# Smaller first transfers with four matmuls on a cleared tile, and later scores, in a two-layer hybrid mixer kernel on one core

## The reference

```python
h = rms_norm(x, pre_g)
proj = h @ w_in              # 2048 x 24576: twelve sections of 1536 columns, three gates of 2048
o_a = dilated_mixture_attn(q_a, k_a, v_a) * silu(z_a)       # 12 heads x 128
o_c = b_c * causal_short_conv(c_c * u_c, conv_w, conv_b) * silu(z_c)
o_r = retention(rotary(q_r), rotary(k_r), v_r) * silu(z_r)  # 12 heads x 128, then normed
merged = sigmoid(g_a) * (o_a @ w_branch_a) + sigmoid(g_c) * (o_c @ w_branch_c) \
       + sigmoid(g_r) * (o_r @ w_branch_r)
x = x + rms_norm(merged @ w_out, post_g)
```

## Time and profile before

| | |
|---|---|
| median of 3 runs | 2788.71 us (2786.34 to 2789.78) |
| the profiled execution | 2791.59 us, its span 2789.7 us |
| PE busy | 2753.0 us (99%) |
| DVE busy | 1845.4 us (66%) |
| ACT busy | 1229.3 us (44%) |
| DMA | 529.11 MB, mean 190 GB/s |

### The profile page before, as it was taken

One profiled execution on the slowest core, in us unless ns is written; L12 is line 12 of the kernel. 1 busy time (PEld: TensorE's weight loads), 2 busy tenths in 40 slices (PEclk: granted clock), 3 DMA queues, 4 the chain that ended last, 5 costly groups with the idle time before them and its releaser, 6 DMA issues.

```text
span 2789.7 us, 30530 instructions
## 1 busy us (share of the span) xinstructions
PE 2753.0 (99%) x12360; PEld 2282.8 (82%) x12360; DVE 1845.4 (66%) x2431; ACT 1229.3 (44%) x1426; POOL 28.2 (1%) x35
## 2 busy tenths in 40 slices
PE   8999999999999999999999999999999999999998
PEld 7888888888888878888878888888888888788887
DVE  5677644767655797746567776447776557877464
ACT  5454544444443333344454545444444433343443
POOL 0000000000000000000000000000000000000000
PEclk9999999999999999999999999999999999999999
DMA  8555556555555555556565555565655564555663
GB/s 312 174 173 195 167 196 196 190 191 194 196 196 193 167 184 170 171 200 213 181 227 178 178 187 167 195 196 182 202 192 194 196 196 156 192 169 171 204 211 136
DMA packets 264108, 529.11 MB, mean 190 GB/s; under 512 B 8352, under 2 KB 8480, under 8 KB 263712
## 3 DMA queue, kind: packets, MB, share of 16 engines
q1 hardware_dynamic: 260208, 517.24, 56.4%
q10 hardware_dynamic: 2752, 5.05, 0.5%
q0 software_dynamic: 1008, 4.87, 0.5%
HBM read 522.94 MB, written 4.19 MB: 189 GB/s over the span
## 4 chain that ended last, share of the span: by engine, by line
PE 98%; issue 1%; DVE 0%; DMA 0%; ACT 0%; DVEq 0%; POOL 0%; ACTq 0%; POOLq 0%
PE ps L585 32%; PE ps L587 32%; PE ps L586 32%; PE ps L516 1%; PE ps L539 0%; PE ps L542 0%; PE ps L540 0%; PE ps L512 0%; PE ps L497 0%; PE ps L526 0%; PE ps L517 0%; PE ps L511 0%; DMA merged<-xT 0%; DVE gates L1082 0%; DVE hT_trail L1054 0%
## 5 line engine op out<-in xcount | busy, mean ns | idle before, releaser
L824 DVE TENSOR_TENSOR w_trail<-raw,w_lead 128x1024 fp32r<-128x1024 f32 x975 | 1191.6, 1225 | 885.1 <-ACT w_lead L644 877.8
L644 ACT ACTIVATE w_lead<-raw 128x1024 fp32r<-128x1024 f32 x975 | 1029.9, 1060 | 1455.7 <-PE ps L587 1445.9
L585 PE MATMUL ps<-w_lead,hT_lead 128*128 128x512 f32 x3328 | 1301.3, 391 | 10.2 <-DVE w_trail L1091 8.7
L587 PE MATMUL ps<-w_lead,hT_trail 128*128 128x512 f32 x3328 | 1296.1, 389 | 0.0
L586 PE MATMUL ps<-w_trail,hT_lead 128*128 128x512 f32 x3328 | 1295.8, 389 | 0.0
L585 PEld LDWEIGHTS ps<-w_lead,hT_lead 128*128 128x128 f32 x3328 | 625.7, 188 | 141.6 <-DVE hT_trail L1073 8.6
L587 PEld LDWEIGHTS ps<-w_lead,hT_trail 128*128 128x128 f32 x3328 | 625.4, 188 | 130.3
L586 PEld LDWEIGHTS ps<-w_trail,hT_lead 128*128 128x128 f32 x3328 | 625.8, 188 | 128.5
L585 PE MATMUL ps<-w_lead,oT_lead 128*128 128x512 f32 x576 | 224.6, 390 | 0.0
L587 PE MATMUL ps<-w_lead,oT_trail 128*128 128x512 f32 x576 | 224.2, 389 | 0.0
L586 PE MATMUL ps<-w_trail,oT_lead 128*128 128x512 f32 x576 | 224.1, 389 | 0.0
(11 more groups left out here) (92 smaller groups left out, 751.9 us busy)
## 6 DMA issues: line engine op xcount, KB each, us to landing
raw<-w_in SPq DMA_DIRECT2D x383, 1024.0 KB, 5.1
raw<-w_out SPq DMA_DIRECT2D x32, 1024.0 KB, 5.1
raw<-w_branch_a SPq DMA_DIRECT2D x24, 1024.0 KB, 5.1
raw<-w_branch_c SPq DMA_DIRECT2D x24, 1024.0 KB, 5.0
raw<-w_branch_r SPq DMA_DIRECT2D x24, 1024.0 KB, 5.0
gates<-x SPq DMA_DIRECT2D x4, 512.0 KB, 14.0
post_gain<-post_norm_g POOLq DMA_DIRECT2D x2, 1024.0 KB, 6.3
gates<-x ACTq DMA_DIRECT2D x4, 512.0 KB, 5.7
```

What stands on the lines that cost most here:

```text
L585: pe.matmul(acc, lead[:, k, tok(t)], wl, start=(k == 0), stop=False)
L587: last = pe.matmul(acc, trail[:, k, tok(t)], wl, start=False, stop=(k == BLOCKS[n][2] - 1))
L644: act.activation(w_lead[:, h % SPLIT_SLOTS, :], raw[:, i % RAW_SLOTS, part:part + HALF * COLS], ACT.Copy).then_inc(lead_ready, 1)
L824: dve.tensor_tensor(w_trail[:, s, :], raw[:, i % RAW_SLOTS, part:part + HALF * COLS], w_lead[:, s, :].bitcast(F32), ALU.subtract).then_inc ...
```

## The change

- **Start.** `XT_PARTS` is cut finer (two parts of one tile, seven of two); SP issues all of them, the first on ACT's queue is gone. The first chunk comes as tile 0, tile 1, tiles 2 and 3, the second chunk as two loads of two tiles, each with its part of x ahead of it. Some x parts wait on SP until an earlier one has landed (`XT_BEHIND`). DVE clears one head of `kT`, and PE runs four float32 matmuls of 256 columns on it ahead of its first half.
- **Residual.** `gates<-x` is issued behind the chunks 5 and 6, two parts each, not behind chunk 3; the squares start at half B+3 and block 0 leaves its banks three halves later. The constants are loaded when PE has done six halves.
- **Scores.** Attention: scores two halves later, exp two later, probs, values, z and out one later. Retention: all one half later. The eviction of the block that follows an attention group (it overwrites `v_sb`) comes one half later on ACT and waits for that group's values.

```diff
-XT_PARTS = ((0, 2), (2, 4), (4, 8), (8, 12), (12, 16))
+XT_PARTS = ((0, 1), (1, 2)) + tuple((k, k + HALF) for k in range(HALF, KT, HALF))
+XT_BEHIND = {2: 0, 3: 1, 4: 2, 5: 3, 7: 5}
+PIECES = 2
+WARM = 4
...
 PE_DUE = due({
-    "attention": [("scores", 3 * B + 6), ("probs", 4 * B + 4), ("values", 4 * B + 6)],
+    "attention": [("scores", 4 * B), ("probs", 4 * B + 5), ("values", 4 * B + 7)],
     "conv": [],
-    "retention": [("scores", 3 * B + 6), ("values", 4 * B + 2)]})
+    "retention": [("scores", 3 * B + 7), ("values", 4 * B + 3)]})
 ACT_DUE = due({
-    "attention": [("exp", 3 * B + 7), ("probs", 4 * B + 4), ("out", 5 * B + 4)],
+    "attention": [("exp", 4 * B + 1), ("probs", 4 * B + 5), ("out", 5 * B + 5)],
     "conv": [("out", 4 * B + 6)],
-    "retention": [("square", 4 * B + 2), ("out", 5 * B + 2)]}, AHEAD)
+    "retention": [("square", 4 * B + 3), ("out", 5 * B + 3)]}, AHEAD)
 DVE_DUE = due({
-    "attention": pieces("q", 2 * B) + pieces("k", 3 * B) + [("scores", 3 * B + 6), ("sums", 4 * B + 3),
-                 ("values", 4 * B + 6)] + pieces("z", 4 * B + 7) + [("out", 5 * B + 5)],
+    "attention": pieces("q", 2 * B) + pieces("k", 3 * B) + [("scores", 4 * B), ("sums", 4 * B + 4),
+                 ("values", 4 * B + 7)] + pieces("z", 5 * B) + [("out", 5 * B + 6)],
...
-    "retention": pieces("q", 2 * B) + pieces("k", 3 * B) + [("scores", 3 * B + 6), ("values", 4 * B + 2),
-                  ("norm", 4 * B + 3), ("gate", 4 * B + 4)] + pieces("z", 4 * B + 5) + [("out", 5 * B + 3)]}, AHEAD)
+    "retention": pieces("q", 2 * B) + pieces("k", 3 * B) + [("scores", 3 * B + 7), ("values", 4 * B + 3),
+                  ("norm", 4 * B + 4), ("gate", 4 * B + 5)] + pieces("z", 4 * B + 6) + [("out", 5 * B + 4)]}, AHEAD)
...
-SQUARES_FROM = B
+VALUES_LATE = 1
+for _n in [first_block("attention", g) for g in range(1, GROUPS)] + [first_block("conv", 0)]:
+    EVICT_DUE[FIRST_HALF[_n + 1] - 1 + AHEAD + VALUES_LATE] = EVICT_DUE.pop(FIRST_HALF[_n + 1] - 1 + AHEAD)
+
+SQUARES_FROM = B + 3
+X_AFTER = {5: (0, 1), 6: (2, 3)}
 EVICT_DUE[SQUARES_FROM + OUT_BLOCKS + 2] = EVICT_DUE.pop(FIRST_HALF[1] - 1 + AHEAD)
...
             def xT_load(part):
                 a, b = XT_PARTS[part]
+                if part in XT_BEHIND:
+                    sp.wait_ge(xT_in[XT_BEHIND[part]], 16)
                 sp.dma_start(xT_sb[:, a:b, :], xT[:, a:b, :]).then_inc(xT_in[part], 16)
...
-                        if l == 0 and i == 0:
-                            raw_load(l, name, tiles, col, c, 0, HALF, i, first_in)
-                            xT_load(1)
-                            raw_load(l, name, tiles, col, c, HALF, CHUNK, i, raw_in[0])
-                            xT_load(2)
+                        if l == 0 and i < PIECES:
+                            if i == 0:
+                                for k in range(HALF):
+                                    xT_load(k)
+                                    raw_load(l, name, tiles, col, c, k, k + 1, i, first_in[k])
+                            else:
+                                xT_load(2 * i + 1)
+                                raw_load(l, name, tiles, col, c, 0, HALF, i, lead_half_in[i])
+                            xT_load(2 * i + 2)
+                            raw_load(l, name, tiles, col, c, HALF, CHUNK, i, raw_in[i])
                             continue
+                        if l == 0 and i < RAW_SLOTS:
+                            xT_load(2 * i + 1)
+                            xT_load(2 * i + 2)
                         sp.wait_ge(trail_ready, l * HALVES + (2 * i + 2))
...
-                        if l == 0 and i + 2 < len(XT_PARTS):
-                            xT_load(i + 2)
-                        elif l == 0 and i + 1 == RAW_SLOTS:
-                            for j in range(OUT_BLOCKS):
+                        if l == 0 and i in X_AFTER:
+                            for j in X_AFTER[i]:
                                 cols = slice(COLS * j, COLS * (j + 1))
                                 sp.dma_start(gates[:, :, cols], x_rows[:, :, cols]).then_inc(residual_in[j], 16)
...
-            pool.wait_ge(half_done, SPLIT_SLOTS + 2)
+            pool.wait_ge(half_done, SPLIT_SLOTS + 6)
...
+            pe.wait_ge(cleared, 1)
+            for _ in range(WARM):
+                pe.matmul(side(SIDE_BANKS - 1)[:, 0:SEQ], kT[:, 0, 0:P], kT[:, 0, :], start=True, stop=True)
...
                         act.wait_ge(*done_block(l, n))
+                        before = {("attention", "v"): j - 1, ("conv", "u"): GROUPS - 1 if j == 0 else -1}.get((mixer, role), -1)
+                        if before >= 0:
+                            act.wait_ge(*step_ready(l, step0("attention", before + 1) - 1))
...
-            act.dma_start(xT_sb[:, 0:HALF, :], xT[:, 0:HALF, :]).then_inc(xT_in[0], 16)
...
-                        if k == 0:
-                            act.wait_ge(first_in, 16)
+                        act.wait_ge(first_in[k], 16)
...
+            dve.memset(kT[:, 0, :], 0.0).then_inc(cleared, 1)
             dve.wait_ge(zeroed, 2 + TILES)
```

More of the change, by code:

```diff
@@ L269, in build @@
         drained = [sem(f"drained{i}") for i in range(SIDE_BANKS)]
-        first_in = sem("first_in")
+        first_in = [sem(f"first_in{k}") for k in range(HALF)]
+        lead_half_in = [sem(f"lead_half_in{i}") for i in range(PIECES)]
+        cleared = sem("cleared")
         xT_in = [sem(f"xT_in{i}") for i in range(len(XT_PARTS))]
@@ L640, in split_lead @@
                 part = (h * HALF % CHUNK) * COLS
-                if part == 0 or (l == 0 and h == 1):
+                if l == 0 and part == 0 and 0 < i < PIECES:
+                    act.wait_ge(lead_half_in[i], 16)
+                elif part == 0 or (l == 0 and i < PIECES):
                     act.wait_ge(*chunk_landed(l, i))
```

## The result

The changed kernel takes 2762.27 us in the median (2760.79 to 2763.0), against 2787.83 beside it: a ratio of 0.9907, with an interval of 0.989 to 0.9924. That is 25.6 us less.

The account below looks back on a forecast made before the run. PE's matmuls bound the kernel (98% of the span), with idle time and low clock to remove. 22.9 + 5.5 + 1.3 + 3.0 = 32.7 us off 2791.6 gives 2758.9, less 2.9 to the median: 2756.0; range 2750.5 to 2763.

Parts of the forecast that it names:

- Retention's scores: Retention's scores one half later: PE's wait for k and the low clock behind it go, 22.9 us saved (bounds 14.9 and 22.9).
- margin of 0.34 us: Retention: PE would reach the scores at 949.33, k is turned at 948.99, so 0.34 us is left over.
- From the profile to the median: Whole kernel: the profiled execution lies 2.9 us above the median, so 2758.9 was lowered to 2756.0.
- Attention's scores: Attention's scores two halves later: groups take 2.60 instead of 3.52 us, 5.5 us saved over six (bounds 4.0 and 5.5).
- Exp: Attention's exp two halves later on ACT: the stall of a 0.49 us matmul goes, 1.3 us saved (bounds 0 and 1.6).
- The start: Kernel start: earlier data and a warmer clock together save 3.0 us (bounds 0 and 3.7, or 6 if supply is faster).
- The gain of the clock: Kernel start: four added float32 matmuls may raise PE's clock before the first half, 0 to 2.7 us.
- supply term: Kernel start: the chunk for tiles 8 to 11 arrives at 15.0 us plus 1, limiting the start's gain to some 3.7 us.
- Rival A: Kernel start gives nothing: small pieces with waits leave DMA engines partly idle, 2759, or 2760 to 2762; chance 0.12.
- B: Retention's wait shrinks but stays because DVE gets to k later: 2760 to 2768; chance 0.10.
- C: Slower than before: work pushed back after the scores arrives late, PE waits at attention's probs, 2790 and more; chance 0.03.
- D: No difference from the scores: the waits are not for k and move along, only the start counts, 2786; chance 0.03.

## Why the prediction came out as it did

**Retention's scores.** Mechanism right, size of the group of waits right in the profiled execution: 22.9 us forecast, 38.50 - 16.47 = 22.0 measured. The margin of 0.34 us held in all six. Two of three groups take 2.8 and not 2.6 us; what holds them for 0.2 us was not looked into.

**From the profile to the median.** This step failed. The prediction took the 2.9 us by which the profiled execution lay above the median for something that stays, and subtracted it from the result. It was the low clock behind retention's wait, four of six times instead of two, and was already contained in the 22.9: the result does not depend on how often the clock fell before. Counted once, the scores save 26.1 us from the median (measured), not 29.7. The profile had the sign of it: the earlier trace rows shows two windows of 5.34 us beside four near 7, a coin that falls differently in each execution (four, two and three low clocks in three executions with these scores).

**Attention's scores.** 5.5 forecast; the six windows went from 21.14 to 15.72, 5.4. **Exp:** right by cause, 1.1 to 1.3 us by its own trace and time. Sum of scores and exp: 29.7 forecast, 29.0 in the profiled execution of the scores alone.

**The start.** Forecast 3.0, measured about zero (0.3 us gained between 2762.55 and 2762.27; at the mark 0.4 lost in one execution and 0.65 gained in another). The first matmul came within the bounds, 5.49 where 5.1 to 6.7 was given, because the parameters landed after 2.6 us instead of 4.1. The gain of the clock came too: high at 6.9 us. What failed is the supply term: "3.0 + 4.6 / 0.385", with 1 us for landing and "two short gaps", where SP has five waits. The chunk landed at 19.5, not 16. I had seen that SP waits for x parts and judged that enough stays queued. But four waits pushed the chunk's issue to 11.01 (4.06 in the kernel before, 8.19 with the waits gone), and the rate from 12 to 16 us was 313 GB/s instead of 390. The fifth wait cannot have held this chunk, which was already queued; what each of the five cost was not run apart. Nor was 16 to be had without them: there the chunk landed at 17.4, and the kernel before already showed later than 16 in ACT's wait for it:

```profile
16.85 1.06 ACT L644 ACTIVATE w_lead<-raw 128x1024 fp32r<-128x1024 f32 x1 [0.96 <-DMA raw<-w_in]
```

By the windows of before some 5.3 MB had moved by then (an estimate from rate times time), 0.5 MB more than the 4.8 of the sum. So the sum was wrong to count nothing beside the transfers up to this chunk: something issued behind it, or other traffic, moved before its end. Which of the two was not looked into.

Rival A had its effect, half 4 at 22 as now, by the waits and not by its own mechanism alone: with the waits gone the small pieces still moved only 284 GB/s from 3 to 8 us, where the old ones had 363 (341 in the run with eleven added matmuls), and 375 to 390 from 8 us on. The rule of the Trainium skill (DMA: Bandwidth & Descriptors, section Bandwidth), to which I gave little weight, so agrees with the trace for the first 8 us, in its direction; how much of it is the size of the pieces, and how much their order and their all being issued by SP, no run separates. I was wrong to read 363 GB/s in a window of 256 KB to 1 MB transfers as an answer for 128 KB ones.

And a step was missing: that PE, run faster through half 0, would idle in front of half 1, whose weights are ready at 11.4 to 12.3 us in every version, small pieces or large. In the kernel before too; VectorE's timeline there, the split of half 1, ends at 10.48 + 1.23 = 11.71:

```profile
10.48 1.23 DVE L824 TENSOR_TENSOR w_trail<-raw,w_lead 128x1024 fp32r<-128x1024 f32 x1 [0.18 <-ACT w_lead L644]
```

The time of half 1 is the bound of the start; half 0 need only be done by then, with the clock high.

**In sum.** 2756.0 forecast, 2762.27 measured, inside the range at its upper end: 2.9 us of it from the median's step, some 3 from the start, 0.9 from retention, the rest small and of both signs. It lies outside the 2750.5 to 2759 that the prediction called its own forecast; the range held because its upper end had been drawn for rivals A and B, and 0.7 us more would have left it. The scores and the exp were right by mechanism and size; that the total was near is owed to them, and not to the start. Rivals B, C and D did not occur.

**The best version.** Small pieces without SP's waits and without added matmuls: 2760.06 us, ratio to before 0.9897 (0.9882 to 0.9911), below both kernels in every run. The intervals of its ratio and of the changed kernel's overlap; that its runs all lie lower (2759.74 to 2760.38 against 2760.79 to 2763.0) and its mark is 3.0 us earlier speaks for a real 2 us, though the two were run in different series.

## What to carry to other kernels

An engine's wait in front of a few instructions can be cured by placing them one step later, where their consumers have time left, and a wait of TensorE costs more than its length when the clock falls behind it; look for windows of the same work with two durations. If a profiled execution lies off the median, find out which term makes the difference before adding or subtracting it, above all when the change removes that term. At the start of a kernel, ask which step's data bounds the engine (here half 1, not half 0), look up in the trace when a transfer landed before dividing bytes by a rate, and keep the transfer queue full; work that only runs the engine earlier into that bound gains nothing.

## What was not expected of the hardware

- The same idle time does not always lower the clock. 2.48 us before retention's scores lowered it in four of six windows in one execution, in two of six and three of six in others; 2.73 us in the changed kernel's start did not, 2.32 us in the run without SP's waits did, and so did 2.44 us in the one with the early residual.
- Matmuls on a tile of zeros raise the clock like others: from 1.92 us on, the spacing of 0.23 us was reached at 6.9 us, 5.0 us after the first of them, against 5.7 us from the first to the last slow matmul in the kernel before. With eleven of them it rose on zeros alone: the 16 instructions from 4.64 to 9.24 us average 0.29 us, against 0.43 at the low level.
- A waiting DMA issue on SP costs rate although much is queued: the fifth wait began with over 1.5 MB still out (an estimate from the issues and the windows), and the DMA engines fell to 195 GB/s between 16 and 18 us of the changed kernel, and returned to 390 with the waits gone.
- With the clock falls in retention gone and all else as before, the scatter of whole executions fell from 6.6 us to 0.5 us.
